# A ring of 24 weight parts in place of 23, with two token tiles' rows kept in PSUM

## The reference

```python
def hier_moe(x, w_rg, b_rg, w_re, b_re, w_gate, w_up, w_down):
    g_logits = (xt @ w_rg + b_rg)                  # 4 groups
    g_idx = jnp.argmax(g_logits, axis=-1)
    e_logits = (xt @ w_re + b_re).reshape(t, N_GROUPS, EXPERTS_PER_GROUP)
    e_sel = jnp.take_along_axis(e_logits, g_idx[:, None, None], axis=1)[:, 0]
    top_v, top_i = lax.top_k(e_sel, TOP_K)         # 2 of 8 experts
    top_w = jax.nn.softmax(top_v, axis=-1) * g_w
    ...
    for gi in range(N_GROUPS):
        h = jax.nn.silu(jnp.einsum('td,edf->tef', xt, w_gate[gi])) * jnp.einsum('td,edf->tef', xt, w_up[gi])
        out = out + jnp.einsum('tef,efd->td', h * combine[:, gi, :, None], w_down[gi])

    x = x + token_mixer(rms_norm(x, norm_mix), ...)
    x = x + hier_moe(rms_norm(x, norm_ffn), ...)
    return rms_norm(x, norm_final)
```

## Time and profile before

| | |
|---|---|
| median of 3 runs | 604.9 us (604.71 to 605.81) |
| the profiled execution's own time | 604.58 us |
| its span | 602.8 us |
| mean granted TensorE clock | 0.994 |
| PE busy | 574.2 us (95%) |
| DVE, ACT, POOL busy | 254.6, 214.5, 61.6 us |
| DMA | 156.02 MB, mean 259 GB/s |

### The profile page before, as it was taken

The page is one execution under the profiler, slowest core; times in us unless marked ns, Lnnn a source line. Parts: engine busy times, 40 slices in busy tenths (PEclk is TensorE's granted clock), DMA queues, the critical chain, the costliest instruction groups (busy, mean ns, idle before and its releaser), DMA issues.

```text
span 602.8 us, 8673 instructions
## 1 busy us (share of the span) xinstructions
PE 574.2 (95%) x3428; PEld 434.6 (72%) x3429; DVE 254.6 (42%) x572; ACT 214.5 (36%) x438; POOL 61.6 (10%) x106
## 2 busy tenths in 40 slices
PE   7999999999999999999999998999999999877885
PEld 4978989888788888888888874766666676544342
DVE  4645677645445765533472375211211211101126
ACT  6634666555786522422152241011111111100114
POOL 3110000001000001100000011012211221111002
PEclk9999999999999999999999999999999999999898
DMA  8365130712231222198789667999999999999996
GB/s 301 87 207 177 58 111 5 291 59 71 71 104 46 61 70 71 37 342 280 291 310 414 246 252 276 380 414 425 422 421 425 424 424 421 425 425 423 425 385 277
DMA packets 59435, 156.02 MB, mean 259 GB/s; under 512 B 8368, under 2 KB 38472, under 8 KB 47744
## 3 DMA queue, kind: packets, MB, share of 16 engines
q1 hardware_dynamic: 54512, 145.74, 63.3%
q0 software_dynamic: 4864, 9.69, 4.2%
q10 hardware_dynamic: 16, 0.00, 0.0%
HBM read 147.31 MB, written 16.27 MB: 271 GB/s over the span
## 4 chain that ended last, share of the span: by engine, by line
PE 76%; DMA 11%; SPq 5%; DVE 4%; ACT 2%; issue 1%; POOL 1%; DVEq 0%; ACTq 0%; POOLq 0%
PE mid_rows L810 17%; PE last_rows L810 16%; PE bank L1247 12%; DMA slots<-expert_w_up 9%; PE bank L810 7%; PE bank L803 5%; SPq L555 5%; PE mid_rows L1267 5%; PE last_rows L868 2%; PE mid_rows L945 2%; DMA w<-w_in 1%; PE mid_rows L868 1%; PE bank L923 1%; PE bank L1118 1%; PE bank L924 1%
## 5 line engine op out<-in xcount | busy, mean ns | idle before, releaser
L1247 PE MATMUL bank<-slots,xgT 128*64 128x256 f32 x544 | 73.0, 381 | 5.2 <-DMA slot2b<-expert_w_up 1.9
L1882 DVE TENSOR_TENSOR w_low<-w,w_high 128x1024 fp32r<-128x1024 f32 x32 | 39.2, 1225 | 78.5 <-ACT w_high L1503 78.5
L1247 PEld LDWEIGHTS bank<-slots,xgT 128*64 128x64 f32 x544 | 49.2, 137 | 23.0 <-issue 4.0
L2237 DVE TENSOR_SCALAR y<-mid_rows,slot_weights 128x512 f32<-128x512 f32 x15 | 11.3, 751 | 99.7 <-PE mid_rows L1267 99.7
L1503 ACT ACTIVATE w_high<-w 128x1024 fp32r<-128x1024 f32 x32 | 33.7, 1054 | 48.6 <-PE last_rows L810 48.6
L1678 ACT ACTIVATE y<-mid_rows,slot_weights 128x512 f32<-128x512 f32 x15 | 10.3, 687 | 95.0 <-PE mid_rows L1267 70.8
L1247 PE MATMUL bank<-slot2b,xgT 128*64 128x256 f32 x240 | 36.6, 381 | 0.2 <-DMA slot2b<-expert_w_up 0.2
L1267 PE MATMUL mid_rows<-slots,hT 128*64 128x512 f32 x112 | 29.1, 594 | 2.6 <-issue 2.6
L1672 ACT ACTIVATE h_silu<-bank 128x256 f32<-128x256 f32 x15 | 5.8, 383 | 72.1 <-PE bank L1247 72.1
L1247 PEld LDWEIGHTS bank<-slot2b,xgT 128*64 128x64 f32 x240 | 23.7, 137 | 7.6 <-issue 1.6
L810 PE MATMUL mid_rows<-x_high,w_high 128*128 128x512 f32 x72 | 28.7, 398 | 0.0
(11 more groups left out here) (424 smaller groups left out, 1368.8 us busy)
## 6 DMA issues: line engine op xcount, KB each, us to landing
slots<-expert_w_up SPq DMA_DIRECT2D x18, 1024.0 KB, 24.3
slots<-expert_w_gate SPq DMA_DIRECT2D x17, 1024.0 KB, 12.8
slots<-expert_w_down SPq DMA_DIRECT2D x15, 1024.0 KB, 24.5
w<-w_in SPq DMA_DIRECT2D x16, 512.0 KB, 3.7
slot2b<-expert_w_up SPq DMA_DIRECT2D x8, 1024.0 KB, 27.2
slot2b<-expert_w_gate SPq DMA_DIRECT2D x7, 1024.0 KB, 16.7
w<-w_in SPq DMA_DIRECT2D x7, 840.0 KB, 4.6
slot2b<-expert_w_down SPq DMA_DIRECT2D x5, 1024.0 KB, 28.9
```

What stands on the lines that cost most here:

```text
L1247: ins = mm(bank[2][e * SLOTS:(e + 1) * SLOTS, m * FE:(m + 1) * FE], xgT[:, c, e * SLOTS:(e + 1) * SLOTS], weights(own, m, e, c * FE, (c + ...
L1882: V.tensor_tensor(wl2[:, u % 2, :], raw2[:, u % 2, :], wh2[:, u % 2, :].bitcast(F32), ALU.subtract).then_inc(s["lo_done"], 1)
L2237: V.tensor_scalar(y_sb[:, 512:1024], bank[5][:, :], weight, None, ALU.mult).then_inc(s["y_outD"], 1)
```

## The change

The ring gets a 24th place, and room is made for it.

- Tile 2's rows stay in PSUM (`mid_rows`) from the output projection on, as tile 3's did: `rows_of` gives them, `residual(2)` writes there. The two copies of the tail (and the semaphore `mid_in`) are gone, and `to_tokens(f, 2, ...)` moves up among the others.
- Banks 4 and 5 are therefore not free for other things. The down products go to banks 0 and 1, where the rows are turned; `turn_x` waits for both halves of the pair before to have left (`rows_out`). The last pair's rows are turned into banks 2 and 3. In the router's stage the banks of the turns, the logits and the ranks are others (`TURNED`, `LT_BANK`), with two new waits in `turn_hn`.
- Tiles 2 and 3 of x2 become a whole buffer, `slot2f`, place 22. The new place 23 is the split part, over three buffers: 1024 words of `fixed`, 512 words behind `hT`, and 512 words of `early`, a buffer in which small operands of the early stages (`rb`, `sink`, `gcol`, `dec`, `selb`, `onesb` and others) now lie together. It is loaded in three pieces. `h_silu` and `h_sb` share memory, `slot_weights` and `by_pair` move.
- Part 23 is issued behind the half parts, once the counts have been taken (`act_done`). The half parts are now 24 and 25.

```diff
-        TURNED = ((0, 1), (2, 3), (4, 5), (3, 5))
+        TURNED = ((0, 1), (2, 3), (0, 2), (3, 0))
-        LT_BANK = {0: 0, 2: 2, 3: 4}
+        LT_BANK = {0: 1, 2: 2, 3: 0}
-        split = (fixed[:, 0:PART // 2], place_at(YB + 3 * D, "slot2f", PART // 2)[:, :])
+        slot2f = place_at(YB + 2 * D, "slot2f", PART)
+        split = (fixed[:, 0:PART // 2], place_at(SMALL + 512, "slot2g", 512)[:, :], early[:, 0:512])
+        SPLIT_AT = (0, PART // 2, PART // 2 + 512, PART)
         ring = (part0 + [behind[4]] + part1 + [slot2a[:, i_ * PART:(i_ + 1) * PART] for i_ in range(2)]
-                + [behind[3]] + behind[0:3] + [slot2c[:, :], slot2d[:, :], slot2e[:, :], split])
+                + [behind[3]] + behind[0:3] + [slot2c[:, :], slot2d[:, :], slot2e[:, :], slot2f[:, :], split])
...
         def rows_of(t):
-            return x2[:, t, :] if t < NT - 1 else last_rows[:, :]
-
-        def summed_rows(t):
             return (x2[:, 0, :], x2[:, 1, :], mid_rows[:, :], last_rows[:, :])[t]
...
                 if ring[q % R] is split:
-                    load_half(q, 0)
-                    load_half(q, 1)
+                    for i, piece in enumerate(split):
+                        cols = slice(SPLIT_AT[i], SPLIT_AT[i + 1])
+                        sp.dma_start(piece, (g_rows, u_rows, d_rows)[m][:, 2 * pair + e, cols]).then_inc(m_in[pair % 4][m], 16)
...
                 sp.wait_ge(s["g_done"], h + 1)
                 for e in range(2):
                     load_half(R + e, h)
+            sp.wait_ge(s["act_done"], 1)
+            load_part(23)
             for q in range(R + 2, 6 * PAIRS):
...
             def turn_hn(t):
                 pe.wait_ge(s["hn_done"], t + 1)
                 for c in range(KC):
-                    if t == NT - 1 and c % 4 == 0:
-                        pe.wait_ge(s["hnT_outD"], 2 + c // 4)
+                    if t == 2 and c % 4 == 0:
+                        pe.wait_ge(s["hnT_outA"], 1 + c // 4)
+                    if t == 3 and c % 4 == 0:
+                        pe.wait_ge(s[("hnT_outD", "hnT_outA")[c // 4]], 2 + c // 4)
...
-            def turn_x(n, k, loads):
+            def turn_x(n, k, loads, rows_out):
                 pe.wait_ge(s[f"gathered{k}"], 16 * loads)
                 for c in range(KC):
+                    if rows_out is not None and c % 4 == 0:
+                        pe.wait_ge(s[("y_outA", "y_outD")[c // 4]], rows_out)
                     ins = tr(bank[c // 4][:, (c % 4) * P:(c % 4 + 1) * P], xv[:, c, :])
...
-                            ins = mm(bank[4 + f][e * SLOTS:(e + 1) * SLOTS, :], hT[:, j, e * SLOTS:(e + 1) * SLOTS],
+                            ins = mm(bank[f][e * SLOTS:(e + 1) * SLOTS, :], hT[:, j, e * SLOTS:(e + 1) * SLOTS],
...
             to_tokens(0, 0, 2, True).then_inc(s["comb_done"], 1)
             to_tokens(0, 1, 3, True)
+            to_tokens(0, 2, 4, False)
             to_tokens(0, 3, 6, False)
-            to_tokens(1, 0, 1, True).then_inc(s["comb_done"], 1)
-            to_tokens(1, 1, 0, True)
+            to_tokens(1, 0, 0, True).then_inc(s["comb_done"], 1)
+            to_tokens(1, 1, 1, True)
+            to_tokens(1, 2, 5, False)
             to_tokens(1, 3, 7, False)
...
-            for f in range(2):
-                pe.wait_ge(s["mid_in"], f + 1)
-                to_tokens(f, 2, 4 + f, False)
...
-            for f in range(2):
-                act.wait_ge(s["ly_lo"], f + 1)
-                A(mid_rows[:, f * 512:(f + 1) * 512], x2[:, 2, f * 512:(f + 1) * 512], ACT.Copy).then_inc(s["mid_in"], 1)
```

More of the change, by code:

```diff
@@ L139, in hybrid_encoder, with early_view @@
         K = {n: cst[:, a:b] for n, (a, b) in CONST.items()}
-        rb = sb("rb", [P, NG + EXPERTS])
-        sink = sb("sink", [P, HEADS])
-        gcol = sb("gcol", [P, KC])
+        early, at_ = sb("early", [P, 540]), 0
+        def early_view(shape, words, dt=F32, rows=P):
+            nonlocal at_
+            at_ += words
+            view = early[0:rows, at_ - words:at_]
+            view = view if dt == F32 else view.bitcast(dt)
+            if len(shape) == 1:
+                return view
+            return view.rearrange("p (a b) -> p a b", b=shape[1]) if len(shape) == 2 else view
+        rb = early_view([NG + EXPERTS], NG + EXPERTS)
+        sink, gcol = early_view([HEADS], HEADS), early_view([KC], KC)
+        dec = early_view([GH, 2 * NT], 2 * GH * NT)
+        between = early_view([GH, NT - 1], GH * (NT - 1))
+        oss, ors = early_view([NT, GH], NT * GH), early_view([NT, GH], NT * GH)
+        selb = early_view([NT, EXPERTS], NT * EXPERTS // 2, BF16)
+        beforeb, onesb = early_view([P], P // 2, BF16), early_view([P], P // 2, BF16)
+        pi = early_view([5, 2 * NT], 10 * NT, I32)
+        cnt = early_view([EXPERTS + PAIRS], EXPERTS + PAIRS, F32, 1)
+        actf = early_view([116], 116, F32, 1)
+        assert 512 <= at_ <= 540
         row_norms = sb("row_norms", [P, 6, NT])
@@ L297, in hybrid_encoder @@
         ZERO_PIECES = 2 * NT
-        arrived = {(n_, m_): sum(32 if q_ in HALVED or ring[q_ % R] is split else 16 for q_, (p_, w_, _) in enumerate(order)
+        arrived = {(n_, m_): sum(16 * len(split) if ring[q_ % R] is split else 32 if q_ in HALVED else 16 for q_, (p_, w_, _) in enumerate(order)
                                  if w_ == m_ and p_ % 4 == n_ % 4 and p_ <= n_) for n_ in range(PAIRS) for m_ in range(3)}
@@ L429, in weights @@
                 return at[:, a:b]
-            return at[a // D][:, a % D:a % D + b - a]
+            piece = max(i for i in range(len(split)) if SPLIT_AT[i] <= a)
+            return at[piece][:, a - SPLIT_AT[piece]:b - SPLIT_AT[piece]]
         def down_rows(n, e, j, f):
@@ L567, in load_half @@
                 cols = slice(h * PART // 2, (h + 1) * PART // 2)
-                sp.dma_start(split[h] if ring[q % R] is split else ring[q % R][:, cols], (g_rows, u_rows, d_rows)[m][:, 2 * pair + e, cols]).then_inc(m_in[pair % 4][m], 16)
+                sp.dma_start(ring[q % R][:, cols], (g_rows, u_rows, d_rows)[m][:, 2 * pair + e, cols]).then_inc(m_in[pair % 4][m], 16)
             sp.wait_ge(s["lo_done"], LOWS)
@@ L1196, in _ @@
             for u in range(NT):
-                ins = mm(bank[4][0:1, P:P + EXPERTS], onesb[:, 0:1], selb[:, u, :], start=(u == 0), stop=(u == NT - 1),
+                ins = mm(bank[3][0:1, P:P + EXPERTS], onesb[:, 0:1], selb[:, u, :], start=(u == 0), stop=(u == NT - 1),
                          skip_group_check=True)
@@ L1677, in y_evac @@
                     act.wait_ge(s[f"scattered{k}"], 16 * waits)
[L1678 removed]
+                A(y_sb[:, 0:512], bank[0][:, :], ACT.Copy, scale=weight).then_inc(s["y_outA"], 1)
             def act_body(n, k, waits, following=True):
```

80 lines of the change are left out of this document (36 added, 44 removed).

## The result

| | median (range), us | runs | span of the profiled run |
|---|---|---|---|
| kernel before | 605.23 (604.71 to 606.47) | 5 | 602.8 |
| changed kernel | 608.82 (608.19 to 610.54) | 5 | 607.0 |

The ratio is 1.0059, with a 95% interval of 1.0039 to 1.0079: the change costs 3.6 us. I had forecast 604.8 within 603.2 to 606.0, so the prediction is wrong, on the side to which it gave 0.14.

What follows compares the result with a forecast made beforehand. The weight stream's end, not TensorE, was taken as the bound. 604.58 - 0.4 (extra part) + 0.3 (pieces) = 604.5 us; with the median 0.3 above the profiled execution, 604.8 us, range 603.2 to 606.0.

Steps and rivals of the forecast that it cites:

- the router's stage: Turns of tiles 2 and 3 ahead of the router's products: two new waits, hidden; cost 0, at most 1.18 us.
- 423 GB/s after 400: Sign of a right forecast: the weight stream still moves 423 GB/s after 400 us.
- The extra part: 24th part issued at about 380.1 us in the load queue: gain 0.4 us, between 0 and 1.56.
- 380 to 400 us would be a little fuller: Sign of a right forecast: the DMA stream in 380 to 400 us moves a little more.
- all later loads keep their times: Load queue behind the new part: later loads keep their releasers and go out at 382.67, 383.04 and on.
- the 6.7 us landing: Load issued at 382.67 lands 6.7 us later though its bytes take 2.48: work is already ahead of it.
- Rival 1: Weight stream: the extra part counts in full, ending it up to 2.48 us sooner, 602.7 us; chance 0.21.
- Three pieces for two: Split part's loads, four in the run, in smaller rows: cost 0.3 us, between 0 and 0.38.
- The price of 8 us: Four more DMAs at a fixed 2.0 us each, one behind the other: 612.9 us; a rival given 0.01.
- The banks: Pair loop's down products in banks 0 and 1: turns get a new wait, margin 2.59 us, cost 0.
- the tail: End of the kernel: two hidden copies of 0.59 us go; gain 0, cost 0, at most 0.5 us either way.
- Rivals 2 and 3: Router's stage later, 606.5 us; pair loop's turns waiting for a scatter, 607 us; together chance 0.11.

Runs made afterwards that it cites:

- e1: Changed kernel with the buffer of early operands 8 words shorter, so the ring lies 32 bytes lower, back on 256-byte lines: 606.02 us, ratio 1.0005 to the kernel before.
- e2: Kernel before with an unused buffer of 8 words (32 bytes) ahead of the placed buffers: 607.85 us, ratio 1.0048.
- e3: Kernel before with an unused buffer of 32 words (128 bytes) ahead of the placed buffers: 607.71 us, ratio 1.0041.
- e5: Kernel before with by_pair laid into the placed region and all placed buffers 256 bytes lower, still on the line: 605.39 us, ratio 1.0003.
- e4: e1 with part 23 and later ones waiting one place further on, never more than 23 parts ahead: 605.61 us, ratio 1.0008 to the kernel before.
- e6: Kernel before with the split part's second half loaded as two loads of 512 words instead of one of 1024: 605.93 us, ratio 1.0009.
- e9: e1 with half of part 22 issued before the wait for gathered rows, the other half and part 23's first piece behind it: 604.20 us, 0.9979 to the kernel before.
- e7: e1 with all of part 22 issued before the wait for gathered rows and part 23's first piece behind it: 606.68 us, ratio 1.0021 to the kernel before.
- e11: Kernel before with slots01 and slot2c, 13 of the ring's 23 parts, placed 32 bytes higher: 606.16 us, ratio 1.0024.
- e12: Kernel before with slots01, slot2c, slot2b and slot2f, 18.5 of the ring's 23 parts, placed 32 bytes higher: 606.99 us, ratio 1.0030.
- e13: Kernel before with by_pair in the placed region, the pair loop's working buffers and two of 23 parts 32 bytes off the line, the rest on it: 608.91 us, ratio 1.0064.
- e8: Kernel before with half of part 22 issued ahead of the wait for pair 0's gathered rows: 605.80 us, ratio 1.0011.

## Why the prediction was wrong

**The step that failed** is the last sentence on the router's stage: "A few operands that move into one early buffer cost nothing." I counted instructions in it, not bytes. The operands cost nothing; the 32 bytes by which they made the small buffers longer moved the placed part of the ring off the 256-byte line, and that cost some 3 us (changed kernel 1.0059, e1 1.0005; the shift alone, e2, 1.0048). I never looked at where the buffers come to lie, though place_at puts everything behind the small ones, and "423 GB/s after 400" stands among my signs as something that nothing in the change could touch.

The Trainium skill has a rule that I should have weighed ("DMA: Bandwidth & Descriptors", how a descriptor splits into AXI transactions): a descriptor that doesn't start on a 256-byte line begins with a transaction from the line below, and what is fetched and not used still costs beats of 32 bytes. The page tells it of what a transaction reads; here the weights are read from HBM as before, and what has moved is where they are written. The trace agrees that the line is one of 256 bytes (e3, e5). Not in the size: by the rule a row of 8 KB that starts 32 bytes past a line would take 257 beats for 256, 0.4%, and one at 128 bytes 260, 1.6%; an estimate worked out from the page. Measured on the packets are 1.6% and 1.2%, the other way round. Nor in the form: the rule would make each packet off the line longer by the same, and 24% of e2's aren't longer at all. So the rule says where to look; how the loss comes about stays open.

**The extra part**, forecast 0.4 us with a low end of 0: it is the low end. e4 without the depth is as fast as e1 with it, and by 400 us the changed kernel had moved 9.56 MB for 9.73 before (e1 9.59). That 380 to 400 us would be a little fuller was wrong. So was the remark that all later loads keep their times: the pieces held the queue for 3.2 us, and the next load went out some 0.7 us after it was due (in e1, 382.73, on time). I had the place right (380 us, a queue with work in it), and chose a number that the 6.7 us landing already spoke against. Rival 1 is gone.

**Three pieces for two**, forecast 0.3 within 0 to 0.38: e6 has 0.5 (0 to 1.1), and 0.13 MB or 0.3 us in 370 to 400. Right as far as it can be told. The price of 8 us, from the fixed 2.0 us a DMA that the Trainium skill gives ("DMA: Bandwidth & Descriptors", anatomy of one DMA), isn't seen; the page fits it to DMAs issued by GpSimd, and these are issued by SyncE.

**The banks, the router's stage, the tail**, forecast 0 each: right. The margin of a turn is 2.59 us as before, the router's products aren't later, and e1, which has all these edits, is within 0.3 us of the kernel before. Rivals 2 and 3 didn't come.

**The sum** for the change without its 32 bytes, 604.8 against a median before of 604.9, agrees with e1, ratio 1.0005 (0.9995 to 1.0016). With -0.4 and +0.3 us its two terms nearly cancel, where the runs have nothing for the first and 0.5 for the second; that the difference stays inside the interval is in part luck. Put together, 2.9 us for the line (e2) and 0.3 for the rest (e1) make 3.2 of the 3.6 measured, inside the interval. No rival had the line, and the range held none of it: the bound that I set on unseen costs came from the engines' rows, and this cost is on none of them.

## What to carry to other kernels

When a kernel lives from a stream of DMA, compute the byte address of its buffers before and after an edit, not only their sizes: a few words more in a small buffer can move all that is allocated behind it. A share of 1.02 with fewer GB/s is the sign: then the bytes themselves have become dearer, and the addresses are to be looked at before order and depth. Before adding a buffer to a stream, look for a moment at which the stream is dry and the buffer can be filled. Where the queue had work in it the 24th part gained nothing (e1 against e4); with an issue moved into the dry moment the kernel was 1.3 us faster than before (e9), but not when a larger one met a transfer that others wait for (e7).

## What the runs showed of the hardware

- Weight rows of 8 KB that start 32 or 128 bytes past a 256-byte line of a partition stream at 417 to 419 GB/s, on the line at 423. Moving 5 of 23 buffers off it costs nothing that can be measured, 13 cost 1 GB/s, 18.5 cost 3.
- In that stream a packet of 8 KB takes 309 ns on the line; off it 24% still do, and the others mostly 313 to 320 (e2). In 285 to 300 us, with other buffers on the line, packets that land off it aren't longer (e11, e12).
- With the buffer of one operand beginning 32 bytes off the line and that of the other on it, products of 128x512 took 395 ns for 389 (e13); with both off, 389 (e2).
- The granted clock falls for some microseconds near 560 us, after TensorE has waited for weights; on which products it falls is worth up to 1.7 us of the end. In three kernels with 423 GB/s it fell on the up products before last, and the last down products began at 584.0 to 584.5 instead of 582.7 (e1, e6, e8). It isn't all of that: in e4 and e7 the clock fell earlier, in 555 to 560 us as before, and they began at 583.8 and 584.0. That it accounts for the scatter of single runs, 604.3 to 608.4 in the kernel before, is likely and wasn't shown.
